# A ConvFFN down-projection over four PSUM banks, a residual product on VectorE, and sums spread over the updates

## What is computed

```
x = layer_norm(ALPHA * x + (1.0 + gate) * mix, ln_g, ln_b)
hin = x * (1.0 + scale) + shift
u = hin @ ffn_w_in + ffn_b_in                      # 1024 -> 2 * 2816
u, hist = causal_dwconv(u, ffn_conv, ffn_conv_w)   # 3 taps
u = u + ffn_conv_b
f = (silu(u[..., :D_FF]) * u[..., D_FF:]) @ ffn_w_down
x = layer_norm(ALPHA * x + (1.0 + gate) * f, ln_g, ln_b)
```

## Time and profile before

| | us |
|---|---|
| three runs | 3169.97, 3170.7, 3174.64 (median 3170.7) |
| the profiled execution | 3175.71 |
| its span in the trace | 3173.9 |
| PE busy | 2951.9 (93%) |
| PEld busy | 2792.6 (88%) |
| DVE busy | 2312.7 (73%) |
| ACT busy | 1227.5 (39%) |
| POOL busy | 986.5 (31%) |

### The profile page before, as it was taken

The page is one execution under the profiler, slowest core; times in us unless marked ns, Lnnn a source line. Parts: engine busy times, 40 slices in busy tenths (PEclk is TensorE's granted clock), DMA queues, the critical chain, the costliest instruction groups (busy, mean ns, idle before and its releaser), DMA issues. The chain is left out here.

```text
span 3173.9 us, 51760 instructions
## 1 busy us (share of the span) xinstructions
PE 2951.9 (93%) x18516; PEld 2792.6 (88%) x18516; DVE 2312.7 (73%) x3500; ACT 1227.5 (39%) x2360; POOL 986.5 (31%) x653
## 2 busy tenths in 40 slices
PE   7999989999998999999998879989998999999995
PEld 5999977999988999999997868878988999999994
DVE  7999966777459777788877556645277788887775
ACT  3333244554345332333333634444155333333224
POOL 2333435665315222223222121110323222222222
PEclk9999989999999999999999999999999999999998
DMA  6545653110111111111111210002201111111111
GB/s 265 176 171 180 227 193 109 54 54 21 54 34 34 47 53 40 45 48 46 46 46 35 90 42 34 35 28 79 78 21 47 41 47 46 48 44 52 41 40 56
DMA packets 86969, 225.75 MB, mean 71 GB/s; under 512 B 9388, under 2 KB 41076, under 8 KB 85812
## 3 DMA queue, kind: packets, MB, share of 16 engines
q1 hardware_dynamic: 46900, 139.10, 12.9%
q10 hardware_dynamic: 39936, 84.86, 7.8%
HBM read 192.59 MB, written 31.35 MB: 71 GB/s over the span
## 5 line engine op out<-in xcount | busy, mean ns | idle before, releaser
L370 POOL TENSOR_TENSOR WL<-RAW,WH 128x1024 fp32r<-128x1024 f32 x193 | 511.5, 2651 | 975.2 <-ACT WH L365 975.1
L374 PE MATMUL PS<-HH,WH 128*128 128x352 f32 x2120 | 704.1, 332 | 61.7 <-POOL WL L370 22.6
L378 PE MATMUL PS<-HH,WL 128*128 128x352 f32 x2120 | 689.8, 325 | 0.0
L377 PE MATMUL PS<-HL,WH 128*128 128x352 f32 x2120 | 689.3, 325 | 0.0
L374 PEld LDWEIGHTS PS<-HH,WH 128*128 128x128 f32 x2120 | 405.4, 191 | 79.4 <-issue 62.4
L2113 DVE SCALAR_TENSOR_TENSOR X<-PS,ADA,X 128x352 f32<-128x352 f32 (+1 forms) x704 | 326.7, 488 | 167.8 <-PE PS L378 162.5
L377 PEld LDWEIGHTS PS<-HL,WH 128*128 128x128 f32 x2120 | 406.4, 192 | 1.8
L378 PEld LDWEIGHTS PS<-HH,WL 128*128 128x128 f32 x2120 | 405.6, 191 | 0.0
L365 ACT ACTIVATE WH<-RAW 128x1024 fp32r<-128x1024 f32 x199 | 210.2, 1056 | 385.7 <-PE PS L374 378.8
L374 PE MATMUL PS<-FH,WH 128*128 128x352 f32 x960 | 325.2, 339 | 28.2 <-DVE X L2113 28.0
L378 PE MATMUL PS<-FH,WL 128*128 128x352 f32 x960 | 310.4, 323 | 0.0
(11 more groups left out here) (384 smaller groups left out, 6281.7 us busy)
## 6 DMA issues: line engine op xcount, KB each, us to landing
RAW<-ws SPq DMA_DIRECT2D x199, 512.0 KB, 3.3
ADR<-wada ACTq DMA_DIRECT2D x72, 512.0 KB, 4.8
scr<-V ACTq DMA_DIRECT2D x32, 528.0 KB, 3.0
X<-xT SPq DMA_DIRECT2D x3, 1408.0 KB, 20.7
OUTT<-scr SPq DMA_DIRECT2D x1, 4224.0 KB, 15.3
y<-X SPq DMA_DIRECT2D x3, 1408.0 KB, 5.5
AD0R<-wada SPq DMA_DIRECT2D x8, 512.0 KB, 13.3
AD<-wada SPq DMA_DIRECT2D x2, 2048.0 KB, 15.1
```

The source lines that it names most:

```text
L370: e.tensor_tensor(WL[u][:, :], RAW[:, u, :], WH[u][:, :].bitcast(fp32), ALU.subtract).then_inc(lo_done, 1)
L374: mm = e.matmul(out, WH[w][:, c:c + 128], mh, start=first, stop=False)
L377: e.matmul(out, WH[w][:, c:c + 128], ml, start=False, stop=False)
L378: return e.matmul(out, WL[w][:, c:c + 128], mh, start=False, stop=last)
```

## The change

Four edits.

1. The three products of the residual by RST leave POOL's list and go to DVE, behind `t_lower(0, 2, 1)` and ahead of `conv(0, 1)`.
2. `down` goes over the banks 6, 7, 1, 5 (`DN_BANKS`), and PE waits for update k - 4 ahead of tile k. New waits: ahead of tile 2, for the last evacuation of the pair by ACT; in `up_mixed(j, 0)`, ahead of the second product (bank 1), for all 24 updates of the down-projection before. `up_first` goes over the banks 0 to 5 in order and `up_mixed(1, 1)` over 1, 2, 3, 4, 0, so that the waits for evacuations there are in the order in which ACT makes them. The last down-projection of a layer (`last`) stays on banks 6 and 7.
3. In `first_half`, DVE's evacuation number 1 is placed ahead of `gate(j - 1, 1)`.
4. `mix` places its eight steps (four `w_sums`, four `sum_lower`) behind the updates 9, 11, 13, ... 23; before, the four `w_sums` stood behind updates 13, 16, 19, 22, and the four `sum_lower` behind the last update. The places of `beside()` are as before (1, 4, ... 22).

```diff
-        def pool_normal(p, q, ch):
+        def vec_normal(v, q, ch):
             c0, cw = CHS[ch]
-            p.wait_ge(hl_rdy, low_count(HS[q], 2))
-            p.tensor_tensor(X[:, :, c0:c0 + cw], X[:, :, c0:c0 + cw], LN_R[q][ch][:, 0:cw].unsqueeze(1).to_broadcast([128, KB, cw]),
+            v.wait_ge(std_rdy, 6 * q + 2 * ch + 2)
+            v.tensor_tensor(X[:, :, c0:c0 + cw], X[:, :, c0:c0 + cw], LN_R[q][ch][:, 0:cw].unsqueeze(1).to_broadcast([128, KB, cw]),
                             ALU.mult).then_inc(nrl_rdy, 1)
...
+        DN_BANKS = (6, 7, 1, 5)
...  up_first
-                    need(e, up_ev, b - 6 + 3 * half + ch + 1)
+                    need(e, up_ev, b - 6 + i + 1)
                     for k in range(KB):
-                        mm = three(e, PS[:, 3 * half + ch, 0:cw], u, k * 128, HH[:, k, c0:c0 + cw], HL[:, k, c0:c0 + cw],
+                        mm = three(e, PS[:, i, 0:cw], u, k * 128, HH[:, k, c0:c0 + cw], HL[:, k, c0:c0 + cw],
...  up_mixed
-                A, C, B, E0, E1 = (5, 2, 3, 4, 0) if f and not head else (0, 1, 2, 3, 4)
+                A, C, B, E0, E1 = (1, 2, 3, 4, 0) if head else (5, 2, 3, 4, 0) if f else (0, 1, 2, 3, 4)
-                free(1, (st_dv, 3 * q - 2))
+                free(3, (st_dv, 3 * q - 2))
+                if not f:
+                    need(e, dn_ev, d0 + 3 * KB * (j - 1))
...  down
-                        need(e, dn_ev, d0 + 3 * KB * j + k - 1)
+                        after(e, dn_ev, d0 + 3 * KB * j + k - 3)
+                        if k == 2:
+                            need(e, up_ev, 3 * (g0 + up_index(j + 1, 1, 0)) + 6)
                         for f in range(2):
-                            mm = three(e, PS[:, 6 + k % 2, 0:cw], u, f * 512 + (m % 4) * 128, FH[:, f, c0:c0 + cw],
+                            mm = three(e, PS[:, DN_BANKS[k % 4], 0:cw], u, f * 512 + (m % 4) * 128, FH[:, f, c0:c0 + cw],
...  pool_ffn
-            pool_normal(p, 2 * l, 0)
             split(n0, 2)
             tails(0, 0)
-            pool_normal(p, 2 * l, 1)
             split(n0, 3)
-            pool_normal(p, 2 * l, 2)
...  vec_ffn
-            def mix(j, steps=iter(()), first=0):
+            def mix(j, steps=iter(()), places=range(1, 3 * KB, 3)):
                 need(v, x_rdy, 6 * l + 3)
                 for k in range(3 * KB):
                     update(j, k, k // 3, k % 3)
-                    if k % 3 == 1 and k >= first:
+                    if k in places:
                         next(steps, None)
...
+            def w_splits(j):
+                yield from w_sums(j, 0)
+                for i in range(4):
+                    sum_lower(j, 0, i)
+                    yield
...
             for i in (0, 2, 1):
                 t_lower(i)
+            for ch in range(NCH):
+                vec_normal(v, 2 * l, ch)
             every_step(conv(0, 1))
...  first_half
                 lower(j - 1, 0)
+                mixed_out(j, 0, 1)
                 gate(j - 1, 1)
-                steps = w_sums(j, 1)
-                next(steps)
-                next(steps)
-                mixed_out(j, 0, 1)
-                every_step(steps)
+                every_step(w_sums(j, 1))
...
-                mix(j - 1, w_sums(j + 1, 0), 13)
-                for i in range(4):
-                    sum_lower(j + 1, 0, i)
+                mix(j - 1, w_splits(j + 1), range(9, 24, 2))
```

More of the change, by code:

```diff
@@ L1697, in up_first @@
                 b = 3 * (g0 + up_index(1, 0, 0))
-                for half, ch in FIRST_ORDER:
+                for i, (half, ch) in enumerate(FIRST_ORDER):
                     if (half, ch) in ((0, 1), (1, 1)):
@@ L1753, in up_mixed @@
                     need(e, st_dv, 3 * q)
-                free(3)
+                elif not head:
+                    need(e, dn_ev, d0 + 3 * KB * (j - 1))
+                free(2)
                 product(A, A11, B11, True, up_done, True)
-                free(1, (st_dv, 3 * q - 2))
+                free(3, (st_dv, 3 * q - 2))
+                if not f:
+                    need(e, dn_ev, d0 + 3 * KB * (j - 1))
                 need(e, sl_rdy, sl_count(l, q, 1))
@@ L1780, in up_mixed @@
                 need(e, lo_done, n + 2)
-                free(2, (up_ev, b))
+                free(1, (up_ev, b))
                 whole(E1, ub)
@@ L1840, in act_ffn, with copy_out @@
             x0, z0 = l * FB, l * (FB + 2)
-            def copy_out(j, f, half, chunks=range(NCH), done=None):
+            def copy_out(j, f, half, chunks=range(NCH), done=None, bank_=None):
                 x = x0 + 2 * j + f
@@ L1853, in copy_out @@
                     need(a, up_done, done or group_at(g, ch))
-                    src = PS[:, 3 * half + ch, :]
+                    src = PS[:, 3 * half + ch if bank_ is None else bank_, :]
                     if c0 + cw <= SEQ:
@@ L1955, in act_ffn @@
                     upper(0, 1)
-                copy_out(1, 0, half, (ch,), b1 + i + 1)
+                copy_out(1, 0, half, (ch,), b1 + i + 1, i)
             def second_half(j, n, first=()):
@@ L2106, in lower, with update @@
                 v.tensor_tensor(FLS[f][:, :], FT[:, f, :], FH[:, f, :].bitcast(fp32), ALU.subtract).then_inc(fl_rdy, 1)
-            def update(j, k, m, ch):
+            def update(j, k, m, ch, banks=DN_BANKS):
                 c0, cw = CHS[ch]
@@ L2112, in update @@
                 for a, w, st in pieces(c0, cw):
-                    ins = v.scalar_tensor_tensor(X[:, m, a:a + w], PS[:, 6 + k % 2, a - c0:a - c0 + w],
+                    ins = v.scalar_tensor_tensor(X[:, m, a:a + w], PS[:, banks[k % len(banks)], a - c0:a - c0 + w],
                                                  ADA[:, s, 2 * KB + m, st:st + 1], X[:, m, a:a + w], ALU.mult, ALU.add)
                 ins.then_inc(dn_ev, 1)
-            def mix(j, steps=iter(()), first=0):
+            def mix(j, steps=iter(()), places=range(1, 3 * KB, 3)):
                 need(v, x_rdy, 6 * l + 3)
@@ L2290, in vec_ffn @@
             second_half(1)
-            mix(0, w_sums(2, 0), 13)
-            for i in range(4):
-                sum_lower(2, 0, i)
+            mix(0, w_splits(2), range(9, 24, 2))
             with v.Fori(2, NP - 1) as j:
@@ L2303, in vec_ffn @@
             last_lower(1, 0)
-            vec_tail(v, 2 * l + 1, lambda ch, m: update(NP - 1, KB * ch + m, m, ch), KB, 2, within())
+            vec_tail(v, 2 * l + 1, lambda ch, m: update(NP - 1, KB * ch + m, m, ch, (6, 7)), KB, 2, within())
         def no_hin(ch):
```

## The result

| | us |
|---|---|
| changed kernel, four runs | 3092.82 to 3094.98, median 3093.64 |
| kernel before, four runs on the same chip | 3169.97 to 3174.64, median 3170.99 |
| ratio | 0.9754, 95% interval 0.9738 to 0.9771 |
| the profiled execution, its span | 3094.34, 3092.5 |

The kernel is 77.35 us faster between medians (2.5%), and 81.4 us between the spans of the two profiled executions, since the one of before lies 5 us above its median. The forecast of 3087 us is 6.6 us too low, and its range holds the time.

A forecast was written before the change was run, and what follows sets the result against it. The prediction took PE as the bound, held up by waits in the FFN. Its terms, 41.4 + 16.5 + 16.6 + 9.0 = 83.5 us, taken from the 3170.7 us median gave 3087 us, range 3072 to 3112 us.

The forecast's parts named there:

- down-projections, 18: Down-projections ahead of each layer's last: four banks and spread sums remove PE's waits, 2.3 us each, 41.4 us in all.
- evacuation: Block (j, 0): evacuation number 1 ahead of the gate removes PE's wait at the last product, 16.5 us.
- heads, 2: Head of each FFN: residual products on DVE gain 12.0 us, less a new 3.7 us loss; 16.6 us in all.
- last down-projections, 2: Each layer's last down-projection: DVE sets its end, 31.06 us become some 26.5; 4.5 us each, 9 in all.
- The queue that I followed: DVE's queue in a down-projection: updates 16, 19, 23 end at 18.4, 20.6, about 24.0 us; no tile waits.
- The gain of DVE's sums: Head of the FFN: without POOL's products DVE's sums end at about 964, not 986; they had cost DVE 22 us.
- The new wait of 3.2 us for slab 5: Second tile of `up_first`: slab 5, behind POOL's tail copies and split, is there at 7.0 us, 3.2 us late.
- The gain of a head that comes out whole: Head of each FFN: PE's 9.21 us wait and the low clock behind it both go, 12.0 us a layer.
- A: Heads: POOL slips its copies between DVE's products, PE never waits there; 95 us gained, 3076 us; chance 0.17.
- B: Next block's second product: PE waits for update 23, or half the evacuation gain is lost; 3102 to 3122 us; chance 0.15.
- C: Whole trip: DVE becomes the bound once PE is faster; gain under 45 us, some 3135 us; chance 0.05.
- D: Down-projection: the first sum, now earlier, waits for a slab not yet landed; slower, 3207 us if 36 us lost; chance 0.02.

The follow-up runs named there:

- only_spread: Kernel before with only the eight steps of `mix` moved behind updates 9 to 23, still two banks; 3156.48 us, ratio 0.9950.
- no_evac: Changed kernel with DVE's evacuation number 1 put back behind the gate and two sums; 3093.52 us, ratio 0.9753.
- neither: Changed kernel with both the spread of the `mix` steps and the earlier evacuation number 1 undone; 3108.95 us, ratio 0.9799.
- wait_split: Changed kernel, DVE waiting for POOL's split of slab 4 ahead of the residual products, the third product behind the convolution; 3084.33 us, ratio 0.9725.
- drop_product: Changed kernel with each of the three residual products cut to 8 columns of one block, output incomplete; 3086.25 us, ratio 0.9727.
- no_spread: Changed kernel with the `mix` steps put back: sums behind updates 13, 16, 19, 22, low halves behind the last; 3094.31 us, ratio 0.9754.
- all_behind: Changed kernel, DVE waiting for POOL's split of slab 4, all three residual products behind the convolution of block (0, 1); 3101.44 us, ratio 0.9774.
- wait_slab4: Changed kernel with DVE waiting for POOL's split of slab 4 ahead of the first residual product; 3092.99 us, ratio 0.9751.
- only_residual: Kernel before with only the three residual products moved from POOL to DVE; 3159.71 us, ratio 0.9961.
- three_banks: Changed kernel with the down-projection over banks 6, 7, 5, PE waiting for update k - 3; 3106.64 us, ratio 0.9788.

## Why the prediction was right, point by point

The mechanism held in the main: PE was the bound, and its waits in the FFN were the price. One gain was given to the wrong edit, and the terms miss by up to 2.8 us each, partly in opposite directions. The terms, from PE's starts:

| term | predicted | measured |
|---|---|---|
| down-projections, 18 | 41.4 | 39.4 (18 x 2.19) |
| evacuation | 16.5 | 15.8 (16 pairs 43.2 to 42.26; 2 of 42.64 to 42.26) |
| heads, 2 | 16.6 | 13.8 (68.50 to 62.03, 68.52 to 61.23) |
| last down-projections, 2 | 9.0 | 10.7 (31.06 to 25.69 in layer 0) |
| sum | 83.5 | 79.7 |

The span shrank by 81.4 us; 1.7 us lie outside these stretches and were not traced. The sum was subtracted from the median too, although it was made against an execution 5 us above it. Between the medians the kernel gained 77.35 us, 4 us less than between the spans; that is most of the 6.6 us by which the forecast was low. The 3081 to 3098 us given for the forecast don't follow from the bounds named with it: a loss of 0.7 to 6.0 us a head and a gain of 0 to 6.6 us a last down-projection give 3077 to 3101 us. The measured time lies in both.

**Down-projection.** Right in place and mechanism; a tile without a wait is 23.24 / 24 = 0.968 us, not 0.963, which makes 2.19 of 2.3 us. The queue that I followed was right to 0.1 us at updates 16, 19 and 23. One sentence of this step was wrong: that any step between updates costs PE nearly its whole length with two banks. only_spread shows that steps of 0.6 us cost 0.1 us at most. Of the 2.2 us in the kernel before, 1.2 were the one step that met POOL's split (the tile behind it takes 2.22 us by PE's starts, not 0.97), some 0.8 the updates in two pieces and 0.2 the other steps. PE's wait there, before:

```profile
1337.43 0.43 PE L374 MATMUL PS<-FH,WH 128*128 128x352 f32 x1 [1.09 <-DVE X L2113]
```

**Evacuation.** Its size was right, its owner was not. The prediction gave all of it to edit 3 and noted only in passing that the low halves had left the start of DVE's trip. By only_spread, no_evac and neither, edit 4 alone does the same, so edit 3 adds nothing to the other three. That the sum came out in spite of it is luck: the change held both edits, and the wait was counted once.

**Residual.** The gain of DVE's sums was right. The new wait of 3.2 us for slab 5 was seen as worked out, in layer 1 of the changed kernel (3.40 us) and in no_evac (3.16 and 3.33); the changed kernel's first head had the worse form, 4.33 us for slab 4. The products also came 3 us earlier than estimated, at 981.76 to 990.84 and not at 985 to 994. Two sizes missed. The gain of a head that comes out whole was taken as 12.0 us; wait_split, the nearest to it, has 57.32 and 57.45 us where 68.50 and 68.52 stood, 11.1 to 11.2 us. The loss was taken as 3.7 us; against wait_split it is 61.23 - 57.45 = 3.8 us in the second head, so right there, and 62.03 - 57.32 = 4.7 us in the first, where the split of slab 4 took 13.90 us. Against drop_product the first head loses 83.16 - 78.10 = 5.1 us. The clock is part of it. In the window behind the wait it is 0.50 (1.2 GHz):

```profile
994.00:995.00 1.00, 1.00 (x5) 1.00 (x5) 1.00 (x2) 1.00 (x2) 0.56 (x2) 0.50 0.76 184
...
997.00:998.00 1.00, 1.00 (x8) 1.00 (x7) 1.00 (x1) 1.00 (x2) 0.77 (x1) 0.94 0.00 0
```

Three such windows cost half their length, 1.5 us, beside the 4.33 - 0.81 = 3.5 us of longer wait: 5.0 us.

**Last down-projection.** DVE sets its end, as forecast. It is busy 23.16 of 24 us (the window's columns as above), and PE waits for its last link:

```profile
1629.00:1653.00 24.00, 22.78 (x141) 22.33 (x139) 23.16 (x40) 4.53 (x7) 4.81 (x2) 1.00 0.14 44
```

```profile
1628.29 0.32 PE L374 MATMUL PS<-FH,WH 128*128 128x352 f32 x1
...
1653.98 0.40 PE L374 MATMUL PS<-HH,WH 128*128 128x352 f32 x1 [2.20 <-DVE HL L2238]
```

The wait grew from 1.34 to 2.20 us, and the stretch took 25.7 us, not the 26.5 taken. The terms that the prediction names for it, 22.9, 1.2 and 1.34 us, give 25.4; for the 1.1 us on top it shows no row.

**Rivals.** A (the head comes out whole) did not happen, but wait_split and drop_product show that it was there to be had by another order. B: PE never waited for update 23, and all pairs of blocks take 42.26 us. C: DVE is not the bound of a trip, which takes 65.50 us where 65.3 were forecast. D: the first sum waited for no slab, it follows update 9 without idle time.

## What to carry to other kernels

When two edits may cover the same wait, test each alone and each taken back: here four edits whose single gains sum to 92.6 us give 77, since two share one. Size the number of banks by the longest thing that can stand once in the consumer's queue, here a step stretched to 1.9 us by another engine, and not by the mean load. An instruction that moves between engines needs its latest place as well as its earliest: look for who consumes it (here ACT's affine), and for what is queued behind that consumer.

## What was unexpected of the hardware

With the products on DVE, POOL's split of slab 4 was issued while T3L ran on DVE, 0.4 to 0.7 us behind T3L's start. In most heads, both of no_spread, no_evac, neither, wait_split and all_behind and the second of the changed kernel among them, it took 3.20 to 3.50 us and T2L waited; in the first heads of drop_product and wait_slab4 T2L went first and the split took 4.91 and 4.97 us; in the changed kernel's first head it took 13.90 us, in only_residual's 13.83 and in the second head of three_banks 13.80, with T2L and all three products ahead of it. The offset from T3L's start doesn't tell them apart (0.45, 0.53 and 0.55 us in the long cases, 0.37 to 0.68 in the others). The Trainium skill (SBUF — State Buffer, "Who interferes with whom") says that issue order decides who blocks. That does not fit the long cases: when DVE's instructions follow each other without a pause, an older POOL instruction may still be passed by several of them. The same held for a copy of 14 elements in all_behind, 9.00 us beside the three products:

```profile
998.99 9.00 POOL L2025 COPY PSF<-PAR 128x14 f32<-128x14 f32 x1 [4.89 <-DVE CF L2089]
```

```profile
998.85 9.08 DVE L629 TENSOR_TENSOR X<-X,RST 128x2816 f32<-128x2816 f32 x3
```

What decides whether POOL gets its turn stays open. A semaphore wait of DVE for the split keeps the products behind it, and none of the six heads with that wait (wait_slab4, wait_split, all_behind) has the long split; of the twelve without it and with the products there, three have.

Of the clock: behind waits of PE of 0.81, 0.91 and 1.03 us the granted clock stayed at full, and behind those of 4.33 and 6.41 us stand windows of 0.50. Between them the length of the wait doesn't tell. In drop_product a wait of 2.20 us had the low clock behind it, and one of 2.94 us, ahead of the first matmul of its second head, had not (PE, then the windows, columns as above):

```profile
1646.20 0.40 PE L374 MATMUL PS<-HH,WH 128*128 128x352 f32 x1 [2.20 <-DVE HL L2238]
...
2310.22 0.40 PE L374 MATMUL PS<-HH,WH 128*128 128x352 f32 x1 [2.94 <-issue]
```

```profile
1647.00:1648.00 1.00, 1.00 (x5) 1.00 (x5) 0.15 (x1) 0.76 (x1) 0.16 (x1) 0.50 0.09 16
...
2311.00:2312.00 1.00, 1.00 (x8) 1.00 (x7) 1.00 (x2) 0.00 (x0) 0.00 (x0) 1.00 0.00 0
```

The changed kernel's first head has a wait of 2.85 us at that place (ahead of 955.63), and the window 957 to 958 behind it is at 0.50. The two heads of drop_product take 78.10 and 76.75 us to `down(0)`, 1.4 us apart, and the low clock in the first is the difference that the trace shows. A difference of that size between two single heads need not be the effect of an edit.
